# A fourth early gate panel, chain steps on half slots, and one group of small products as eight full-width ones, in the gated-delta stage of a ten-stage kernel

## The reference, cut to what matters

```
proj = x @ w_in                                  # 1024 -> 4096 (q, k, v) + 2048 (z) + 32 gates
qkv  = silu(causal_depthwise_conv(qkv, conv_w))  # width 4
...
a     = where(strict, (k*beta) @ k.T * decay, 0)       # one matrix for each of 16 heads and each chunk
t_inv = triangular_solve(eye + a, eye, lower=True)
u, w  = t_inv @ (v*beta),  t_inv @ (k*beta*exp(g))
step over chunks: v_new = u - w @ state;  o = q_g @ state + qk @ v_new;  state = decayed state + k_tail.T @ v_new
o = rms(o) * norm_w * silu(z);   out = o @ w_out
```

## Time and profile before

| | us |
|---|---|
| median of 3 timed runs | 1987.55 (1983.15, 1987.55, 1987.73) |
| the profiled execution, its own time | 1986.61 |
| its span | 1984.8 |
| delta stage in it, slots 0 to 46 | about 1510 to 1736 |
| TensorE busy | 1956.2 (99%) |
| VectorE busy | 1397.1 (70%) |
| ScalarE busy | 1101.6 (55%) |

### The profile page before, as it was taken

How to read it: one execution, slowest core, us unless ns; L and a number is a source line. 1 busy time by engine, 2 the same in 40 slices (tenths; PEclk the granted TensorE clock), 3 DMA queues, 4 the chain that set the end, 5 groups by cost and what they waited for, 6 DMA issues and landing times.

```text
span 1984.8 us, 41590 instructions
## 1 busy us (share of the span) xinstructions
PE 1956.2 (99%) x15610; PEld 1823.6 (92%) x15610; DVE 1397.1 (70%) x2394; ACT 1101.6 (55%) x1845; POOL 122.0 (6%) x204
## 2 busy tenths in 40 slices
PE   8999999999999999999999999999999899999998
PEld 7999899989999999999999999999999899989998
DVE  6688877766788877666667765575557978477655
ACT  5665555556654655554454544454447878556443
POOL 2031000000040000000000000000000333000000
PEclk9999999999999999999999999999999899999999
DMA  9433665544335555465546455555554544445552
GB/s 313 151 128 128 222 208 189 187 171 149 129 122 187 204 188 187 151 213 190 190 154 216 149 203 190 186 173 190 184 189 162 184 123 134 151 159 199 185 188 95
DMA packets 118248, 348.49 MB, mean 176 GB/s; under 512 B 23336, under 2 KB 35960, under 8 KB 117744
## 3 DMA queue, kind: packets, MB, share of 16 engines
q1 hardware_dynamic: 115392, 335.23, 49.4%
q0 software_dynamic: 2736, 11.59, 1.8%
HBM read 340.81 MB, written 5.96 MB: 175 GB/s over the span
## 4 chain that ended last, share of the span: by engine, by line
PE 89%; DVE 5%; ACT 4%; issue 1%; DMA 0%; SPq 0%; DVEq 0%; ACTq 0%
PE bank L2420 28%; PE bank L2422 27%; PE bank L2421 27%; DVE wlo L1603 1%; ACT whi L1024 1%; PE bank L2734 1%; ACT xhi L1040 1%; DVE arena L1671 1%; DVE conv L2134 1%; PE bank L2456 1%; PE bank L2707 0%; ACT psq L1048 0%; PE bank L2926 0%; PE bank L2695 0%; DVE xlo L1614 0%
## 5 line engine op out<-in xcount | busy, mean ns | idle before, releaser
L2420 PE MATMUL bank<-xhi,whi 128*128 128x256 f32 x3368 | 958.2, 285 | 7.1 <-DVE wlo L1603 3.0
L2421 PE MATMUL bank<-xlo,whi 128*128 128x256 f32 x3368 | 943.5, 280 | 1.1 <-issue 1.1
L2422 PE MATMUL bank<-xhi,wlo 128*128 128x256 f32 x3368 | 942.9, 280 | 0.0
L1603 DVE TENSOR_TENSOR wlo<-raw,whi 128x1024 fp32r<-128x1024 f32 x621 | 750.5, 1231 | 199.6 <-ACT whi L1024 196.9
L2420 PEld LDWEIGHTS bank<-xhi,whi 128*128 128x128 f32 x3368 | 635.3, 189 | 21.1 <-DVE wlo L1603 4.0
L2421 PEld LDWEIGHTS bank<-xlo,whi 128*128 128x128 f32 x3368 | 635.9, 189 | 7.0 <-issue 1.3
L1024 ACT ACTIVATE whi<-raw 128x1024 fp32r<-128x1024 f32 x621 | 632.4, 1045 | 12.3 <-DMA raw<-panels 6.6
L2422 PEld LDWEIGHTS bank<-xhi,wlo 128*128 128x128 f32 x3368 | 635.3, 189 | 0.0
L2420 PE MATMUL bank<-whi,hhi 128*128 128x512 f32 x688 | 272.8, 396 | 0.5 <-DVE hlo L1794 0.5
L2422 PE MATMUL bank<-whi,hlo 128*128 128x512 f32 x688 | 271.0, 394 | 0.0
L2421 PE MATMUL bank<-wlo,hhi 128*128 128x512 f32 x688 | 270.3, 393 | 0.0
(11 more groups left out here) (393 smaller groups left out, 1744.2 us busy)
## 6 DMA issues: line engine op xcount, KB each, us to landing
raw<-panels SPq DMA_DIRECT2D x621, 512.0 KB, 3.6
arena<-w_in POOLq DMA_DIRECT2D x2, 2048.0 KB, 10.5
arena<-relay SPq DMA_DIRECT2D x8, 512.0 KB, 5.5
arena<-gains_in POOLq DMA_DIRECT2D x6, 512.0 KB, 4.0
relay<-arena POOLq DMA_DIRECT2D x4, 512.0 KB, 8.2
relay<-arena SPq DMA_DIRECT2D x4, 512.0 KB, 3.5
x<-x_in SPq DMA_DIRECT2D x1, 1024.0 KB, 5.0
arena<-bias_table POOLq DMA_DIRECT2D x8, 128.0 KB, 7.4
```

The source lines that it names most:

```text
L1603: dve.tensor_tensor(wlo[slot][:], raw[slot][:], whi[slot][:].bitcast(F32), ALU.subtract) \
L2420: pe.matmul(dst, w_hi, a_hi, start=start, stop=False, skip_group_check=True)
L2421: pe.matmul(dst, w_hi, a_lo, start=False, stop=False, skip_group_check=True)
L2422: return pe.matmul(dst, w_lo, a_hi, start=False, stop=stop, skip_group_check=True)
```

## The change

Three things, all in the delta stage:

1. `EARLY_Z` is 4: one more gate panel comes early, in slot 11. All tiles of sets 1, 2 and 3 and their steps come one slot later, set 3's last link ends in slot 46 rather than 45, and the arena has 256 more columns for that gate.
2. `CHAIN` names for each link a step and a half (MIDDLE or END), one function per engine issues all links, and links are moved: set 0's t16 from the end of slot 17 to the middle of 18, u16 and w32 from the middle of 18 to its end, t32 from the end of 18 to the middle of 19, o from the end of 25 to the middle of 26. Sets 1 and 2 have up to three half slots more between links; set 3 keeps its spacing.
3. t16 is eight products of 128x128 by 128x16 for a set, one for each matrix, where it was 32 of 32x32. The other blocks of the operands are zero.

```
-Z, EARLY_Z = 15, 3
+Z, EARLY_Z = 15, 4
-Z_AT = {3: 0, 6: 1, 9: 2, **{LAST + f: f for f in range(EARLY_Z, Z)}}
+Z_AT = {3: 0, 6: 1, 9: 2, 11: 3, **{LAST + f: f for f in range(EARLY_Z, Z)}}
-CHAIN = ({"w16": 13, "t16": 13, "u16": 14, "w32": 14, "t32": 14, "w64": 15, ...
-AMID = (("w16", "u16", "w32"), ("w16", "u16"), ("w16", "u16"), ("w16", "u16", "w32", "w64", "s1"))
+MIDDLE, END = 0, 1
+CHAIN = ({"w16": (13, MIDDLE), "t16": (14, MIDDLE), "u16": (14, END), "w32": (14, END), "t32": (15, MIDDLE), ...
-ROOT_AT = 43
+ROOT_AT = 44
-SCALED_AT = {44: (0, 1), 45: (2, 3), 46: (4, 5)}
+SCALED_AT = {45: (0, 1, 2), 46: (3, 4, 5)}
...
 def delta_t16(n):                    # TensorE
...
                 for m in range(MATS):
-                    for r in range(4):
-                        ks = slice(32 * r, 32 * r + 32)
-                        last = pe.matmul(bank[6][ks, BLK * m:BLK * (m + 1)], tt[ks, m, ks], w16[ks, m, :],
-                                         start=True, stop=True)
+                    last = pe.matmul(bank[6][:, BLK * m:BLK * (m + 1)], tt[:, m, :], w16[:, m, :], start=True, stop=True)
...
+            def delta_chain(n, o, half):     # one on each engine
+                here = lambda step: CHAIN[n][step] == (o - late(n), half)
+                if here("w16"):
+                    delta_w16(n)
...
```

More of the change, by code:

```diff
@@ L1549, in delta @@
                     for n in range(SETS):
-                        delta_amid_result(n, set_step(t, n))
+                        delta_chain(n, set_step(t, n), MIDDLE)
                     if t > 0 and t in TILE_AT:
@@ L1556, in delta @@
                     for n in range(SETS):
-                        delta_result(n, set_step(t, n))
+                        delta_chain(n, set_step(t, n), END)
                     if t - 1 in TILE_AT:
@@ L2337, in delta_o_scaled, with delta_chain @@
                                       .to_broadcast([P, nk, P]), ALU.mult).then_inc(d["o_scaled"], 1)
+            def delta_chain(n, o, half):
+                here = lambda step: CHAIN[n][step] == (o - late(n), half)
+                if here("w16"):
+                    delta_w16(n)
+                if here("t16"):
+                    delta_t16(n)
+                if here("u16"):
+                    delta_u16(n)
+                if here("w32"):
+                    delta_w32(n)
+                if here("t32"):
+                    delta_u32(n)
+                if here("ks"):
+                    delta_v1_in(n)
             def delta_step(s, n, o):
@@ L2352, in delta_step @@
                     delta_qmat(n)
[L2353 to L2361, removed]
+                delta_chain(n, o, END)
+                if p == CHAIN[n]["o"][0] + 2 and n + 1 < SETS:
                     delta_o_added(n)
@@ L3046, in delta_o, with delta_chain @@
                         last.then_inc(d["o_sum"], 1)
+            def delta_chain(n, o, half):
+                here = lambda step: CHAIN[n][step] == (o - late(n), half)
+                if here("w16"):
+                    delta_w16(n)
+                if here("t16"):
+                    delta_t16(n)
+                if here("u16"):
+                    delta_u16(n)
+                if here("w32"):
+                    delta_w32(n)
+                if here("t32"):
+                    delta_t32(n)
+                if here("w64"):
+                    delta_w64(n)
+                if here("u64"):
+                    delta_u64(n)
+                if here("r0"):
+                    delta_r0(n)
+                if here("s1"):
+                    delta_s1(n)
+                if here("ks"):
+                    delta_ks(n)
+                if here("r1"):
+                    delta_r1(n)
+                if here("o"):
+                    delta_o(n)
             def delta_step(s, n, o):
@@ L3062, in delta_step @@
                     delta_turn_v(n, p - 9)
[L3063 to L3067, removed]
-                    delta_t32(n)
-                if p == CHAIN[n]["w64"] and "w64" not in AMID[n]:
-                    delta_w64(n)
-                if p == CHAIN[n]["u64"]:
-                    delta_u64(n)
-                if p == CHAIN[n]["r0"]:
-                    delta_r0(n)
-                if p == CHAIN[n]["s1"] and "s1" not in AMID[n]:
-                    delta_s1(n)
-                if p == CHAIN[n]["ks"]:
-                    delta_ks(n)
-                if p == CHAIN[n]["r1"]:
-                    delta_r1(n)
-                if p == CHAIN[n]["o"]:
-                    delta_o(n)
+                delta_chain(n, o, END)
             def delta(s):
```

47 lines of the change are left out of this document (20 added, 27 removed).

## The result

The change made the kernel slower. Medians of twelve runs each: 1991.24 us (1988.64 to 1996.16) after, 1985.56 us (1981.83 to 1987.87) before, ratio 1.0034, 95% interval 1.0025 to 1.0044. A second measurement, beside the experiments, gave 1.0035 (1.0023 to 1.0047). The forecast was 1984.0, range 1978.5 to 1990: the time lies outside it and on the other side.

What follows compares the result with a forecast made beforehand. TensorE, busy 99%, bounds the kernel; only its waits, low clock or work matter. t16 +3.1, set 0 +0.7, result waits -1.05, issue -3.6, second low clock -1.3, end -0.5: -2.65 on 1986.61 gives 1984.0, range 1978.5 to 1990.

Steps and rivals of the forecast that it cites:

- t16, +3.1: t16 as eight wide products takes 1.04 us more a set; hidden in set 0, sets 1 to 3 pay 3.1.
- the issue waits, -3.6: TensorE's issue waits of 1.0, 1.1 and 1.5 us in sets 1, 2 and 3 all go.
- The rival by which the issue waits stay: Issue waits belong to ends of instruction blocks, so the 3.6 us are not saved: 1987.6; chance 0.13.
- Set 0, +0.7: Set 0's chain: ScalarE stands idle before the turned copy, waits grow, the clock falls; slot 20 begins 0.7 us later.
- the 3 us that the prediction names as a sign of being wrong: In set 0, TensorE's waits before t16, w32 and t32 summing to under 3 us would show the prediction wrong.
- the two walks: Set 0's timeline to slot 20: starting at 1592.4 at full clock, at 1595.7 with low clock from about 1577 to 1591.
- Spread links end these waits: Sets 1 to 3: 0.5 us of the state's wait goes, o's 1.2 falls to 0.65: -1.05 with both.
- a second low stretch that goes: With set 3's issue wait, its 3.4 us at the lower clock go: -1.3 us.
- The slower rival: Slots 18 to 21: a second low-clock stretch of 13.7 us follows: 1989.5, or 1993.1 with issue waits kept; chance 0.13.
- The wait behind the stage (L1794): TensorE's 0.5 us wait for VectorE's scaling at the stage's end goes: -0.5, bounds -0.5 and +0.6.

Runs made afterwards that it cites:

- One entry of the table: The changed kernel with t32 of sets 1 and 2 half a slot earlier (end of step 14, not middle of 15): 1984.57 us, 0.9999 to the kernel before.
- repaired kernel: Changed kernel with three edits together: set 0's turned copy one slot later, t32 (sets 1, 2) half a slot earlier, set 0's o half a slot later: 1979.72 us, 0.9979.
- the spread alone: Changed kernel without the fourth gate panel and with t16 in 32 quarters, so only the moved links are left: 1986.27 us, 1.0007 to the kernel before.
- the gate alone: Kernel before with only the fourth gate panel in slot 11, old chain table and t16 as 32 products a set: 1987.17 us, 1.0014.

## Why the prediction was wrong

- **t16, +3.1, and the issue waits, -3.6.** Right. L2934 has 16 records a set and took 1.7 to 1.8 us to the next start (in set 0 1.8), and no issue wait is left. Alone the edit gave -1.6 where these two terms and set 0's issue wait of 1.0 give -1.5. The rival by which the issue waits stay falls. So does what the prediction drew from the Trainium skill (Runtime: NRT & Kernel Launch, § Instruction fetch mechanics), where crossing from block to block is mostly hidden, so that fewer instructions would give nothing. The measurement contradicts the skill itself only if these waits are such crossings, which no run shows.
- **Set 0, +0.7.** ScalarE did stand idle before L1444 (5.0 us, not 3 to 4), and the decays ended at 1573.1 where the prediction has 1572.7. But "Queued behind it: two slots' taps and `whi`, the silu" was followed to VectorE alone; the silu is also what TensorE needs for keys x keys of set 1, and there it waited 3.25 us. The wait was not added to the others, it took the place of the 1.79 for the inverses and of part of the rest: the waits before t16, w32 and t32 were 1.5, 0 and 1.2 against 2.1, 0.8 and 1.6. By the letter their sum of 2.7 is under the 3 us that the prediction names as a sign of being wrong, and with the one before keys x keys it is 6.0 where the walk has 6.3. With 3.4 us of low clock, not 13, slot 20 began at 1593.05, between the 1592.4 and 1595.7 of the two walks and 1.95 sooner than before (0.4 of that stood already at the stage's start). So here the term erred in the other direction, -1.55 for +0.7, and the loss came behind slot 20.
- **The step that failed: "Spread links end these waits" (-1.05).** The waits that it names went as forecast: that for the state is gone, and o of set 1 has 0.67 for the forecast 0.65. But the term puts at nothing the waits that the new order makes. w64 of sets 1 and 2 waits 2.9, since the table moved t32 half a slot nearer to it, and a table load, a silu and o's two copies (2.8 us) stand ahead of t32's copy on ScalarE. o of set 0 waits 2.0, since the gate, not the spread, put u16 of set 1 half a slot ahead of it; on VectorE the additions of t16, a read and three taps stand ahead of u16's copy. Together that is +4.9 against the term.
- **The clock (-1.3 for a second low stretch that goes).** It went, but two others came. The prediction looked for the fall of the clock in set 0 only. Waits of 1.5 to 2 us in o of set 0 and w64 of set 1 were followed by 3.4 us at 0.50 each, and in most executions there was more. The slower rival had the right mechanism, a second low stretch behind set 0's chain. In the first profile it fell in set 1's chain instead; in the second 10.1 of 23.9 us lay at the end of slot 19 and in slot 20, where the rival has it.
- **The account, in the profiled execution.** Behind slot 20 the prediction has -3.35 (3.1, -1.05, -3.6, -1.3, -0.5). Measured: TensorE began slot 20 1.95 us sooner than before and the next stage 1.66 later (1742.25 against 1740.59), so +3.6. Of the 7.0 between them 4.9 are the waits above, and the 6.8 us of new low clock at 0.4 to 0.5 give an estimated 3. The wait behind the stage (L1794) is gone, as forecast.
- **The range.** Its upper end came from low clock in one place and the issue waits kept. A case in which the distances of sets 1 to 3 turn out too short was missing altogether, and it is what happened.

Shown: the standstill and the wait in o of set 0 are the gate's (there with it alone). One entry of the table, which takes away w64's waits, is worth as much as the whole loss, though it is not the only place: o half a slot later gives 4.8 us by the ratios, and the three edits together 11. In the changed kernel the clock falls behind waits in which TensorE stands, and does not when all of them are filled; in the repaired and the old kernel some low clock stayed with the longest waits filled. Only argued: why the parts do not add up. The waits account for about half of the 4 us between sum and whole (sum of parts +1.7, -3.9 and +1.5 in waits, whole +1.1), the rest would be the clock or the uncertainty of the ratios.

## What to carry to other kernels

A distance in a table of steps is worth what stands ahead of the copy on its own engine: before a product is moved nearer to its reader, list that engine's queue between them. When an engine is to stand idle, follow everything queued behind it, to every reader. And price a wait of TensorE not by its length alone: here one entry of a table that took away two waits of 1.5 us gave 6.9 us, and by the clocks of the runs about half of that is low clock that went with them.

## What was not expected of the hardware

- A wait filled with idle products can cost less than an empty one: 37 products of ones in the waits of the changed kernel made it 6.3 us faster and drew its runs together from 7.5 us apart to 0.5 for ten of eleven. In the repaired kernel the same gave 1.5 us, within the intervals, and in the kernel before nothing.
- The same program with the same waits had 10.2 us of low clock in one execution and 23.9 in another, and a low stretch behind keys x keys of set 1 in one and not in the other. A single profile doesn't price it.
- Issue waits come and go with the number and the order of the instructions: 4.6 us in the kernel before, 5.7 with the spread alone, 1.6 with the gate alone, none in any kernel with eight wide products per set.
- A 128x128 product of 16 columns takes two records of about 0.11 us, 1.7 to 1.8 us for a set of eight. Twice the row of 128 columns gives 1.6, so here an eighth of the columns made it no cheaper.
